# Sample attention over cached keys: order of its DMA requests, which engine scales the probabilities, and where the keys are split

## The reference, cut to what matters

```python
ckv_all = concatenate([past_ckv, ckv_new], axis=1)        # 8 streams x (512 + 16) x 256
k_rope_all = concatenate([past_kr, kr_new], axis=1)       # 8 x 528 x 32
kvb = (ckv_all @ w_kv_b).reshape(b, S, 16, 64 + 64)
k_nope, v = rmsnorm(kvb[..., :64], k_norm), kvb[..., 64:]
s = (einsum('bqhd,bkhd->bhqk', q_nope, k_nope)
     + einsum('bqhr,bkr->bhqk', q_rope, k_rope)) * ATTN_SCALE
p = softmax(s, axis=-1)
o = einsum('bhqk,bkhd->bqhd', p, v)
```

## Time and profile before

| what | before |
|---|---|
| median of three runs | 2051.49 us |
| lowest and highest of them | 2044.13 and 2052.73 us |
| the profiled execution | 2044.24 us |
| its span in the trace | 2042.4 us |
| TensorE busy | 1889.3 us (93% of the span) |
| VectorE busy | 1144.4 us (56%) |
| ScalarE busy | 827.3 us (41%) |
| GpSimd busy | 245.0 us (12%) |
| TensorE's share of the chain that ended last | 81% |
| mean granted TensorE clock, share of full speed | 0.961 |

### The profile page before, as it was taken

One profiled execution on the slowest core, in us unless ns is written; L12 is line 12 of the kernel. 1 busy time (PEld: TensorE's weight loads), 2 busy tenths in 40 slices (PEclk: granted clock), 3 DMA queues, 4 the chain that ended last, 5 costly groups with the idle time before them and its releaser, 6 DMA issues.

```text
span 2042.4 us, 28316 instructions
## 1 busy us (share of the span) xinstructions
PE 1889.3 (93%) x10584; PEld 1777.2 (87%) x10584; DVE 1144.4 (56%) x1733; ACT 827.3 (41%) x1427; POOL 245.0 (12%) x315
## 2 busy tenths in 40 slices
PE   9999998999998999999999999999854479999997
PEld 9999997889878999999999998766654469999997
DVE  6555457778779555447655444556543335555444
ACT  5333246546454333335533323554432234333333
POOL 1000112020220000014000011400121103000011
PEclk9999998999999999999999999999977789999999
DMA  5444443535524444443444444201143223444441
GB/s 199 127 129 125 141 159 119 196 109 206 193 76 147 141 128 127 133 139 112 133 131 128 130 135 169 77 21 42 34 121 83 73 64 123 129 125 123 135 144 62
DMA packets 67779, 249.71 MB, mean 122 GB/s; under 512 B 9480, under 2 KB 10760, under 8 KB 66416
## 3 DMA queue, kind: packets, MB, share of 16 engines
q1 hardware_dynamic: 54000, 196.67, 30.7%
q0 software_dynamic: 13696, 51.90, 8.1%
HBM read 235.74 MB, written 12.12 MB: 121 GB/s over the span
## 4 chain that ended last, share of the span: by engine, by line
PE 81%; DVE 8%; ACT 5%; DMA 3%; issue 2%; POOL 1%; SPq 0%; ACTq 0%; DVEq 0%; POOLq 0%
PE pair L1751 22%; PE pair L1752 22%; PE pair L1753 22%; PE pair L2246 2%; DMA lowA<-in_cacheT 2%; PE pair L2167 1%; DVE wlo L1141 1%; PE pair L1758 1%; PE pair L1760 1%; PE pair L1759 1%; PE pair L1948 1%; ACT seg L801 1%; ACT kn L1010 1%; PE pair L1967 1%; PE pair L2169 1%
## 5 line engine op out<-in xcount | busy, mean ns | idle before, releaser
L1751 PE MATMUL pair<-xh,whi 128*128 128x384 f32 x1960 | 664.2, 339 | 15.2 <-DVE xl L1151 13.3
L1753 PE MATMUL pair<-xh,wlo 128*128 128x384 f32 x1960 | 657.7, 336 | 0.0
L1752 PE MATMUL pair<-xl,whi 128*128 128x384 f32 x1960 | 657.5, 335 | 0.0
L1141 DVE TENSOR_TENSOR wlo<-raw,whi 128x1024 fp32r<-128x1024 f32 (+3 forms) x372 | 463.4, 1247 | 181.0 <-ACT whi L672 172.4
L672 ACT ACTIVATE whi<-raw 128x1024 fp32r<-128x1024 f32 (+2 forms) x369 | 378.8, 1029 | 296.5 <-PE pair L1753 282.3
L1751 PEld LDWEIGHTS pair<-xh,whi 128*128 128x128 f32 x1960 | 370.5, 189 | 25.7 <-issue 14.9
L1752 PEld LDWEIGHTS pair<-xl,whi 128*128 128x128 f32 x1960 | 370.4, 189 | 1.8 <-issue 1.2
L1753 PEld LDWEIGHTS pair<-xh,wlo 128*128 128x128 f32 x1960 | 369.9, 189 | 0.0
L1751 PE MATMUL pair<-ah,whi 128*128 128x384 f32 x704 | 237.0, 337 | 3.5 <-DVE tu L1162 3.3
L1752 PE MATMUL pair<-al,whi 128*128 128x384 f32 x704 | 236.5, 336 | 0.0
L1753 PE MATMUL pair<-ah,wlo 128*128 128x384 f32 x704 | 236.5, 336 | 0.0
(11 more groups left out here) (400 smaller groups left out, 2413.0 us busy)
## 6 DMA issues: line engine op xcount, KB each, us to landing
raw<-in_stream SPq DMA_DIRECT2D x372, 512.0 KB, 3.6
S<-in_ssm POOLq DMA_DIRECT2D x4, 2048.0 KB, 9.1
out_ssm_s<-S POOLq DMA_DIRECT2D x4, 2048.0 KB, 8.0
seg<-acs_rows POOLq DMA_DIRECT2D x12, 512.0 KB, 4.8
cTb<-in_cacheT POOLq DMA_DIRECT2D x10, 512.0 KB, 4.0
kn<-rs_rows POOLq DMA_DIRECT2D x16, 264.0 KB, 7.3
lowC<-in_cache POOLq DMA_DIRECT2D x8, 512.0 KB, 3.5
lowA<-in_cacheT POOLq DMA_DIRECT2D x6, 512.0 KB, 6.1
```

The source lines that it names most:

```text
L1141: V.tensor_tensor(wlo[:, r, 0:w], raw[:, r, 0:w], whi[:, r, 0:w].bitcast(F32), ALU.subtract).then_inc(lo_ready, 1)
L1751: M(out, whi[:, r, ws], mh_(k), start=first and k == k0, stop=False)
L1752: M(out, whi[:, r, ws], ml_(k), start=False, stop=False)
L1753: ins = M(out, wlo[:, r, ws], mh_(k), start=False, stop=last and k == k1 - 1)
```

## The change

The change has five edits.

- **First requests.** The store of the norms of streams 0 to 5 (`rs_past`, which waits for `rs_ev`) moves behind the requests of `wkT`, of stream 0's keys and of its rotary keys.
- **Order of requests.** In the loop over units, the norms of unit `u` come first. Keys and rotary keys of stream `b + 2` follow the norms of the even unit `2b`, and the values of stream `b` follow the norms of the odd unit `2b + 1`. Keys and rotary keys of stream 2 come ahead of the loop.
- **Scaling.** The product of the probabilities with the reciprocal of their sum moves from VectorE to ScalarE (`s_scale(u)`), behind the exponential of the unit. VectorE makes the reciprocal, and a new semaphore `p_sum_ready` hands it over.
- **Split on VectorE.** `keys_split(b)` moves behind the `s_max` of an even unit: for stream 1 it comes behind the `s_max` of unit 1 and not ahead of it, and for stream `b` from 2 on behind that of unit `2b - 2`, where it came behind that of unit `2b - 3`.
- **Small ones.** In the prompt attention the two subtractions for the rotary queries move from head 6 (behind items 1 and 3) to heads 6 and 8 (behind item 1 each). TensorE waits for `filled` to reach 5 ahead of the first scores, which was set long ago.

```diff
             for b in range(STREAMS):
...
-            pool.wait_ge(rs_ev, 2)
-            pool.dma_start(rs_past(0, 6, 0, 3 * P), rsT[0:6 * MH, :]).then_inc(rs_st, 16)
-            pool.dma_start(rs_past(0, 6, 3 * P, P), rsT2[0:6 * MH, 0:P]).then_inc(rs_st, 16)
             for x in range(0, MH, MH // 4):
                 pool.wait_ge(qk_ps, x + MH // 4)
                 pool.dma_start(wkT[0:QD, x:x + MH // 4], T["wkT"][:, x:x + MH // 4]).then_inc(wkT_ld, 16)
...
             past_keys(0)
             past_rope(0)
+            pool.wait_ge(rs_ev, 2)
+            pool.dma_start(rs_past(0, 6, 0, 3 * P), rsT[0:6 * MH, :]).then_inc(rs_st, 16)
+            pool.dma_start(rs_past(0, 6, 3 * P, P), rsT2[0:6 * MH, 0:P]).then_inc(rs_st, 16)
             past_keys(1)
...
             past_rope(1)
+            past_keys(2)
+            past_rope(2)
             for u in range(2, UNITS):
-                b = u // 2 + 1
-                if u % 2 == 0 and b < STREAMS:
-                    past_keys(b)
-                    past_rope(b)
+                b = u // 2
                 if u == 12:
                     pool.wait_ge(rs_st, 16 * 5)
                 past_rstd_rows(u)
-                if u % 2 and b < STREAMS:
+                if u % 2 == 0 and b + 2 < STREAMS:
+                    past_keys(b + 2)
+                    past_rope(b + 2)
+                if u % 2 and b >= 2:
                     past_values(b)
...
+            def s_scale(u):
+                s, o = u % 2, 64 + 8 * (u % 2)
+                act.wait_ge(p_sum_ready, u + 1)
+                A(Pb[:, s, 0:KEYS], Pb[:, s, 0:KEYS], ACT.Copy, scale=sm[:, o + 5:o + 6]).then_inc(p_ready, 1)
...
             s_exp(0)
+            s_scale(0)
             keys_split(1)
             for u in range(UNITS):
...
                 if u + 1 < UNITS:
                     s_exp(u + 1)
+                    s_scale(u + 1)
...
             s_max(0)
-            keys_split(1)
             for u in range(UNITS):
                 s, o = u % 2, 64 + 8 * (u % 2)
                 dve.wait_ge(s_exp_ready, u + 1)
-                step(V.reciprocal(sm[:, o + 5:o + 6], sm[:, o + 4:o + 5]))
-                V.tensor_scalar(Pb[:, s, 0:KEYS], Pb[:, s, 0:KEYS], sm[:, o + 5:o + 6], None, ALU.mult).then_inc(p_ready, 1)
+                V.reciprocal(sm[:, o + 5:o + 6], sm[:, o + 4:o + 5]).then_inc(p_sum_ready, 1)
                 if u + 1 < UNITS:
                     s_max(u + 1)
-                if u % 2 == 0 and 2 <= u // 2 + 2 < STREAMS:
+                if u == 0:
+                    keys_split(1)
+                elif u % 2 and u // 2 + 2 < STREAMS:
                     keys_split(u // 2 + 2)
```

More of the change, by code:

```diff
@@ L374, in build @@
         p_max_ready = sem("p_max_ready")
+        p_sum_ready = sem("p_sum_ready")
         p_exp_ready = sem("p_exp_ready")
@@ L1666, in _ @@
                         V.reciprocal(ksq[:, :, 2 * i:2 * i + 2], ksq[:, :, 2 * i:2 * i + 2]).then_inc(past_rstd, 1)
-                    if x == 6 and i in (1, 3):
-                        y = (xh, xl)[i // 2]
+                    if x in (6, 8) and i == 1:
+                        y, b0 = ((xh, 0), (xl, 4))[x // 8]
                         dve.wait_ge(rope_ld, 80)
                         V.tensor_tensor(y[NOPE:QD, :, SEQ:TOK],
-                                        Qs[NOPE:QD, 4 * (i // 2):4 * (i // 2) + 4, :, :].rearrange("p b h q -> p (b h q)").rearrange(
+                                        Qs[NOPE:QD, b0:b0 + 4, :, :].rearrange("p b h q -> p (b h q)").rearrange(
                                             "p (k c) -> p k c", k=KD), y[NOPE:QD, :, SEQ:TOK].bitcast(F32),
@@ L2215, in _ @@
             pe.wait_ge(qc_ev, 8)
+            pe.wait_ge(filled, 5)
             pe.wait_ge(rs_ev, 3)
```

## The result

The changed kernel takes 1997.03 us (median of 4 runs, 1991.99 to 1998.42); the kernel before, run beside it, 2049.07 us (4 runs, 2044.13 to 2052.73). The ratio is 0.9743, with a 95% interval from 0.9714 to 0.9772. The forecast was 2005, with a range from 1988 to 2025. The profiled execution after is one of 1998.42 us.

What follows compares the result with a forecast made beforehand. The prediction took TensorE's waits in the sample attention, from a ring of key and value requests, as the bound. From 2044.24 us, 9.0 + 36.0 - 2.1 - 0.3 = 42.6 gave 2001.6; median put at 2005, range 1988 to 2025.

Steps and rivals of the forecast that it cites:

- the new ring: Sample attention: norms' landing, next scores, even unit's `s_max`, split and norms' request take 18.2 us per stream instead of 23.7.
- The waits for products, for keys: Sample attention, sign of being right: GpSimd's 115.8 us for products and ScalarE's 51.0 us for keys gone.
- the waits for `kn`: Sample attention, sign of being right: VectorE waits for the norms in each stream, some 8 us at a time.
- the scores at the low clock: Sample attention: scores ahead of the even unit's `s_max` priced at 3.58 us, against 2.09 at the full clock.
- The landing: Sample attention: norms' request to use taken as 7.4 us at seven units on the path, minus 2.1 us of gain.
- the gain from the first scores to unit 15: Sample attention: 36.0 us from the request order and the split, before deductions for landings and scaling.
- The first rival: Sample attention: norms land in 5.5 us or clock stays full; both 1984 us, one 1992 to 1997; chance 0.14.
- The start: Ahead of the first scores: requesting `wkT` and stream 0's keys earlier removes ScalarE's 8.96 us wait, gaining 9.0 us.
- The subtraction: Prompt attention, heads 6 and 8: moving the subtractions for rotary queries gains zero, plus or minus 1 us.
- The scaling: Sample attention: on ScalarE it is covered by the norms' landing, except at unit 15, where it costs 0.3 us.
- The sum: Whole kernel: 9.0 + 36.0 - 2.1 - 0.3 = 42.6 us gained.

Runs made afterwards that it cites:

- N: Changed kernel with the odd unit's norms requested ahead of the next keys and rotary keys, no longer behind them; 1982.53 us.
- D: Changed kernel with four GpSimd fills ahead of the norms of units 3, 5, 7, 9 and 11, requesting them 2.6 us later; 2001.88 us.
- U1: Changed kernel with the first requests back in the old order, the store of the norms ahead of `wkT` and stream 0's keys; 2004.08 us.
- O5: Kernel before the change with only the second rotary-query subtraction moved from head 6 to head 8; 2039.92 us.
- U3: Changed kernel with VectorE scaling the probabilities again instead of ScalarE; 1992.54 us.
- U34: Changed kernel with VectorE scaling again and its split of the keys back behind the odd units; 1984.21 us.

## Why the prediction was right, and where it was not

**The bound and the new ring: right.** The waits for products, for keys and for the scaled probabilities all but went, the waits for `kn` came at 6.4 to 9.2 us, and unit 1 started 5.7 us after the first scores, as forecast. All pieces of the ring but the landing came within 0.13 us. That includes the scores at the low clock: 5.09 us from unit 3 to unit 4, forecast 1.50 + 3.58. N removes the ring's cause and 17 us with it, so the ring was the bound.

**The landing: mis-sized.** I took 7.4 us for each of seven. The six that carry the path to unit 11 took 4.99, 5.39, 6.36, 5.84, 7.74 and 4.66, together 9.4 us less than six times 7.4. That makes the gain from the first scores to unit 15 42.6 us instead of 33.9. The seventh, unit 14's, is not on the path: VectorE waited there for TensorE's scores. I had taken the price from landings of the old order, most of which had the values of a stream ahead as well and all the second norms right behind, and added to it. D shows that a landing depends on what is still under way. Why these six are shorter than the old ones stays open, though: unit 3 has the same neighbours in the new order as unit 2 had before (keys 1.8 us ahead, nothing else near, the next norms 0.6 us behind), and it landed in 5.3 us where unit 2 took 7.0. The first rival, with 5.5 us and a chance of 0.14, was nearer on this term. The Trainium skill (DMA: Bandwidth & Descriptors, "Anatomy of one DMA") gives an estimate of 2.6 us for such a transfer. The trace disagrees: even in D, where the keys have landed, it takes 4.03 to 4.53 us to the use, and unit 15's norms in N, requested 5 us behind GpSimd's request ahead of them, land in 3.8.

**The start: 7.65 of 9.0 us.** ScalarE's wait did go, and its keys were split 9.05 us earlier, counted from the last request (44.22 and 35.17 us). But I followed ScalarE alone. TensorE's 64 products with `wkT`, which before started 1.7 us ahead of ScalarE's split, start 0.2 us behind it now:

```profile
1479.06 9.01 PE L2220 MATMUL pair<-Qs,lowA 96*128 96x128 f32 x64 [1.78 <-DVE xl L1686]
```
```profile
1482.21 0.66 ACT L1072 ACTIVATE whi<-pair 128x256 fp32r<-128x256 f32 x2 [1.05 <-PE pair L2220]
```

They are no longer released by `wkT` but by VectorE, and ScalarE waits for them. Only 7.15 us were to be had there. Without the edit, but with the subtraction moved, the stretch takes 56.25 us in U1 and 56.26 in O5, which is 1.2 longer than in the kernel before; from the first of the 64 products on it is 13.3 and 13.2 us at a granted clock of 0.76, against 12.5 at 0.84 before. Against those two the edit is worth 8.9 us.

**The subtraction: wrong.** I had put it at 0, plus or minus 1. I counted VectorE's time, which moved from one head to another, and overlooked that the two places were not alike: with two in the same head TensorE waited and lost clock, 2.9 us, and with one at head 8 nothing shows.

**The scaling: right in the ring, small at the end.** 0.35 us lie between before and after behind unit 15, forecast 0.3; U3 puts the price in the new order at 1.3.

**What was not asked.** The prediction took edits 2 and 4 as one and priced their ring. It had the piece in hand, 5.08 us for the next unit ahead of the split, and didn't ask what the ring would be without it. U34 answers with 11 us. Whether the split can be moved alone, with the scaling on ScalarE and the split in its old place, was not tried: ScalarE would wait for the reciprocal behind a split that waits for ScalarE.

**The sum.** The stretches with an edit gained 52.8 us in the profiled executions (2.9 + 7.65 + 42.6 - 0.35); the forecast was 42.6. Chance took 6.9 us back. That 52.0 us lie between the two medians is nearer to the first number. The median is 8 us below the forecast, for which the range left 17: the landings and the subtraction gave more than forecast, and the start less.

## What to carry to other kernels

When a request is moved to start sooner, write down what now stands behind it in the same list: the large keys went ahead of the small norms, and the norms became the bound; the small transfer that is needed next goes first. After a ring is named, ask of each of its pieces who put it there, as a piece may come from another edit of the same change, and undoing that one edit is the cheaper gain. A landing read from the trace holds for what was under way beside it, and it scatters: in a new order it is a range and not a number.

## What the runs showed of the hardware

- The landing of the same 264 KB depends on what is still under way: from request to use 4.25 us (4.03 to 4.53) when the keys' 512 KB were requested 4.4 us before, and 6.00 (4.66 to 7.74) at 1.8 to 2.2 us before. With 256 KB more between, the 6.56 (5.06 to 8.15) are within the scatter of the second. The Trainium skill (DMA: Bandwidth & Descriptors, "Queues, rings and completion order") says that each DMA engine works its descriptors off in the order of the ring; it states this for the queues of the engines SP and ACT, and these requests are GpSimd's. The shorter landing in D fits. As a whole a transfer can still be overtaken: the values requested 0.6 us behind unit 9's norms took 6.5 us and those norms 7.7.
- One instruction of 1.22 us on VectorE, beside a busy TensorE, cost 2.9 us: 1.3 of idle time and 1.6 because the products ran at a granted clock of 0.91, on average, instead of 1.00.
- The same products can fall into a low or a full stretch of the clock. In the kernel after, the first unit's scores had a granted clock of 1.00 (2.4 GHz) and unit 4's, after 2.22 us of idle time, 0.50 (1.2 GHz). In U1 the first unit's had 0.50 as well, which cost it some 1.3 us beside the 8.9. What decides it is not shown. N has the same list as the kernel after up to these scores, with the same idle times of TensorE ahead of them (0.8, 1.8 and 2.6 us). There the products with `wkT` ran faster and the first scores slower, and from the first of those products to VectorE's first operation it is 14.1 us in both. The windows are of the kernel after (first unit, unit 4), of U1 (first unit), and then from `wkT` to the first scores of the kernel after and of N:

```profile
1491.10:1493.10 2.00, 1.93 (x14) 1.71 (x14) 0.00 (x0) 0.00 (x0) 2.00 (x4) 1.00 0.14 33
1520.70:1524.10 3.40, 3.40 (x15) 3.40 (x16) 0.87 (x3) 2.39 (x6) 0.00 (x0) 0.50 0.00 0
```
```profile
1494.60:1497.00 2.40, 2.40 (x11) 2.40 (x12) 0.00 (x0) 0.00 (x0) 2.16 (x4) 0.50 0.26 56
```
```profile
1479.06:1491.08 12.02, 9.45 (x69) 9.16 (x69) 8.95 (x20) 8.63 (x22) 3.98 (x8) 0.86 0.64 179
```
```profile
1481.87:1492.63 10.76, 8.09 (x69) 7.61 (x69) 8.64 (x20) 8.58 (x22) 3.98 (x8) 0.98 0.68 200
```
